# K of group B and q, k of group C made token by token in three products; weights split ahead of the norm's last steps; norm in two steps a tile; PSUM copies moved to ScalarE

## The reference, cut to what matters

```
h = rms_norm(x, norm1)
z = h @ w_in                      # 1024 -> 3072 columns
za, bq, bk, bv, cq, ck, cv, cg = split(z)   # 512, 512, 512, 512, 256, 256, 256, 256
a_out = causal_spatial_gating(gelu(za), ...)      # layer norm of half of za, then a 128x128 mix in time
b_out = dilated_attention(heads(bq), heads(bk), heads(bv))   # 8 heads x 64
c_out = silu(cg) * group_norm(retention(rotary(cq), rotary(ck), cv))   # 4 heads x 64
x = x + concat([a_out, b_out, c_out]) @ w_out
x = x + hier_moe(rms_norm(x, norm2))   # 16 experts, top 2 of one group of 4
```

## Time and profile before

| | us |
|---|---|
| median of 3 runs (lowest, highest) | 730.98 (730.19, 731.46) |
| profiled execution, its own time | 730.64 |
| its span (first to last instruction) | 728.8 |
| PE busy | 684.9 (94%) |
| DVE busy | 285.9 (39%) |
| ACT busy | 178.3 (24%) |
| DMA, mean over the span | 331 GB/s |
| mean granted TensorE clock | 0.988 |

### The profile page before, as it was taken

One profiled execution on the slowest core, in us unless ns is written; L12 is line 12 of the kernel. 1 busy time (PEld: TensorE's weight loads), 2 busy tenths in 40 slices (PEclk: granted clock), 3 DMA queues, 4 the chain that ended last, 5 costly groups with the idle time before them and its releaser, 6 DMA issues.

```text
span 728.8 us, 8951 instructions
## 1 busy us (share of the span) xinstructions
PE 684.9 (94%) x3408; PEld 394.7 (54%) x3408; DVE 285.9 (39%) x583; ACT 178.3 (24%) x332; POOL 16.0 (2%) x29
## 2 busy tenths in 40 slices
PE   6999999899999999997999999989999999998884
PEld 5888778733543543432488878776353453442331
DVE  2439986711231121221453698874121320221224
ACT  3216434211301311101140535442121122101102
POOL 3000000200000000000020000000000000000000
PEclk9999999999999999999999999998999999999998
DMA  9964129999999999999985330897999998999991
GB/s 338 337 237 146 39 99 386 378 387 411 410 418 409 381 420 421 420 420 423 401 277 190 136 116 30 327 389 279 424 402 422 411 424 355 423 421 421 420 411 64
DMA packets 46025, 240.95 MB, mean 331 GB/s; under 512 B 3456, under 2 KB 3648, under 8 KB 21280
## 3 DMA queue, kind: packets, MB, share of 16 engines
q1 hardware_dynamic: 44800, 238.21, 81.3%
q0 software_dynamic: 1040, 2.04, 1.2%
q10 hardware_dynamic: 144, 0.13, 0.1%
HBM read 239.32 MB, written 1.05 MB: 330 GB/s over the span
## 4 chain that ended last, share of the span: by engine, by line
PE 73%; DMA 14%; DVE 9%; ACT 2%; issue 1%; DVEq 0%; SPq 0%; ACTq 0%
PE psum L1012 25%; DMA up_w<-in_w_up 13%; PE psum L715 13%; PE psum L1043 12%; PE psum L735 4%; PE psum L742 4%; PE psum L995 3%; PE psum L956 3%; DVE piece_lo L1111 2%; PE psum L941 1%; PE psum L883 1%; PE psum L700 1%; DVE scores L1148 1%; PE psum L1024 1%; DMA x<-in_x 1%
## 5 line engine op out<-in xcount | busy, mean ns | idle before, releaser
L1012 PE MATMUL psum<-up_w,xT 128*64 128x512 f32 x512 | 113.8, 594 | 8.9 <-DMA up_w<-in_w_up 8.9
L1043 PE MATMUL psum<-down_w,scores 128*64 128x512 f32 x512 | 113.4, 595 | 0.6 <-ACT scores L649 0.6
L715 PE MATMUL psum<-piece_hi,hT_part 128*128 128x512 f32 x288 | 90.6, 396 | 0.6 <-DVE piece_lo L1111 0.6
L1012 PEld LDWEIGHTS psum<-up_w,xT 128*64 128x64 f32 x512 | 37.1, 137 | 82.2 <-issue 66.2
L1443 DVE TENSOR_TENSOR y_lo<-psum,y_hi 128x512 fp32r<-128x512 f32 x32 | 22.1, 692 | 134.1 <-ACT y_hi L656 134.1
L1043 PEld LDWEIGHTS psum<-down_w,scores 128*64 128x64 f32 x512 | 36.6, 137 | 64.6 <-issue 62.4
L1012 PE MATMUL psum<-gate_a,xT 128*64 128x512 f32 x256 | 56.9, 594 | 4.6 <-DMA gate_a<-in_w_gate 4.6
L715 PEld LDWEIGHTS psum<-piece_hi,hT_part 128*128 128x128 f32 x288 | 53.0, 188 | 12.3 <-DVE piece_lo L1111 1.5
L1012 PE MATMUL psum<-gate_b,xT 128*64 128x512 f32 x256 | 56.4, 593 | 0.0
L715 PE MATMUL psum<-piece_lo,hT_part 128*128 128x512 f32 x144 | 56.3, 391 | 0.0
L1428 DVE SCALAR_TENSOR_TENSOR work<-work,psum 128x512 f32<-128x512 f32 x16 | 11.0, 688 | 108.1 <-ACT work L647 108.1
(11 more groups left out here) (240 smaller groups left out, 841.8 us busy)
## 6 DMA issues: line engine op xcount, KB each, us to landing
up_w<-in_w_up SPq DMA_DIRECT2D x32, 2048.0 KB, 13.9
down_w<-in_w_down SPq DMA_DIRECT2D x64, 1024.0 KB, 11.8
gate_b<-in_w_gate SPq DMA_DIRECT2D x32, 1024.0 KB, 13.1
gate_a<-in_w_gate SPq DMA_DIRECT2D x32, 1024.0 KB, 15.4
up_w<-in_w_in SPq DMA_DIRECT2D x6, 2048.0 KB, 11.1
down_w<-in_w_in SPq DMA_DIRECT2D x4, 2048.0 KB, 20.7
down_w<-in_w_out SPq DMA_DIRECT2D x4, 2048.0 KB, 7.8
up_w<-in_w_in SPq DMA_DIRECT2D x4, 1024.0 KB, 8.4
```

Source lines behind the costliest of these rows:

```text
L715: ins = pe.matmul(o, src[a][:, c, t * P:(t + 1) * P], w[b][:, c, :], start=(c == 0 and n == 0), stop=(c == DC - 1 and n == len(parts) - 1))
L1012: ins = pe.matmul(psum[e * SLOTS:(e + 1) * SLOTS, bank, :], xT[:, c, k:k + SLOTS], w[:, e, c, :], start=(c == 0), stop=(c == DC - 1))
L1043: ins = pe.matmul(psum[e * SLOTS:(e + 1) * SLOTS, 2 + n, :], heT[:, c, e * SLOTS:(e + 1) * SLOTS], down_w[:, e, c, n * COLS:(n + 1) * COLS ...
```

## The change

1. BK and CQK go through `three_products` too, tokens on partitions. ACT and DVE split both pieces (4 more halves each; `piece_hi1` is now used by BK, CQK, BV and 7). ACT copies the two token tiles out of PSUM into `vb` with the factor `rstd_in` (`copy_tokens_of`), and PE turns them into features on partitions, 8 transposes each (`turn_tokens`): those of BK between ZA's two token tiles, those of CQK after `turn_probs(0)`. One copy of 1024 columns then takes each result out of PSUM, DVE for K of B, ACT for q and k of C. PE's wait for the masked mixing weights moves ahead of ZA, since the transposes reuse PSUM bank 7.
2. The row of factors is gone with all that made it: `spread`, the product with ones, three DVE products and a copy; the rotary products read the tables themselves.
3. On DVE `norm_probs(0)` stands ahead of the layer norm's last steps, and these are two chained steps on each token tile (four of 128x256) where there were two of 128x256 and two of 128x512. Both low halves of CVG follow each other.
4. The copy of k of C and the middle third of the probabilities' copy go from DVE to ACT.
5. The first `hT` lies in the room of `probsT` (`hT_first`), since the second high buffer covers `hT`.

```diff
-        SPLIT = {ZA: 0, CVG: 1, BV: 2, 6: 3, 7: 4}
-        HI_BUFFER = {ZA: 0, CVG: 0, BV: 1, 6: 0, 7: 1}
-
-        HI_AFTER = {CVG: ZA + 1, BV: CQK + 1, 6: CVG + 1, 7: BV + 1}
+        SPLIT = {BK: 0, ZA: 1, CQK: 2, CVG: 3, BV: 4, 6: 5, 7: 6}
+        HI_BUFFER = {BK: 1, ZA: 0, CQK: 1, CVG: 0, BV: 1, 6: 0, 7: 1}
+
...
+                def copy_tokens_of(j, k):
+
+                    act.wait_ge(projected.sem, projected.at(l, j + 1))
+                    for t in range(T):
+                        ins = act.activation(vb[:, t, :], psum[:, PIECE_BANK[j] + t, :], ACT.Copy, scale=rstd_in[:, t:t + 1])
+                    ins.then_inc(tokens_copied.sem, 1)
+
...
-                    for b in (0, 2):
+                    for b in (range(3) if k == 0 else (0, 2)):
...
-                act.activation(hT_parts[0][:], hT[:], ACT.Copy).then_inc(hT_hi_ready.sem, 1)
+                act.activation(hT_parts[0][:], hT_first, ACT.Copy).then_inc(hT_hi_ready.sem, 1)
+                split_hi(BK)
                 act.wait_ge(projected.sem, projected.at(l, BQ + 1))
                 act.activation(qkb[:, 0:2, :], psum[:, 0:2, 0:SEQ], ACT.Copy).then_inc(proj_copied_a.sem, 1)
                 split_hi(ZA)
+                act.wait_ge(rstd_in_ready.sem, rstd_in_ready.at(l, 1))
+                copy_tokens_of(BK, 0)
+                split_hi(CQK)
                 copy_piece(ZA, za[:, 0, :], rstd_in[:, 0:1])
...
-                copy_piece(CQK, qkc[:, 0:2, :].rearrange("p c t -> p (c t)"))
+                copy_tokens_of(CQK, 1)
                 copy_probs(0)
+                act.wait_ge(tokens_turned.sem, tokens_turned.at(l, 2))
+                act.activation(qkc.rearrange("p c t -> p (c t)"), psum[:, PIECE_BANK[CQK]:PIECE_BANK[CQK] + 2, :].rearrange("p b n -> p (b n)"),
+                               ACT.Copy).then_inc(proj_copied_a.sem, 1)
...
-                    elif j in (BK, CQK):
-
-                        for m in range(4):
-                            o = psum[:, bank + m // 2, (m % 2) * SEQ:(m % 2 + 1) * SEQ]
-                            for c in range(DC):
-                                ins = pe.matmul(o, w[:, c, m * P:(m + 1) * P], hT[:, c, :], start=(c == 0), stop=(c == DC - 1))
-                            if m == 3:
-                                ins.then_inc(projected.sem, 1)
...
+                def turn_tokens(k, bank):
+
+                    pe.wait_ge(tokens_copied.sem, tokens_copied.at(l, k + 1))
+                    for m in range(4):
+                        for t in range(T):
+                            ins = pe.transpose(psum[:, bank + m // 2, (2 * (m % 2) + t) * P:(2 * (m % 2) + t + 1) * P],
+                                               vb[:, t, m * P:(m + 1) * P], ident)
+                    ins.then_inc(tokens_turned.sem, 1)
...
-                pe.wait_ge(spread_ready.sem, spread_ready.at(l, 1))
-                pe.matmul(psum[:, 6, 0:SEQ], C("ones"), spread, start=True, stop=True).then_inc(rstd_spread.sem, 1)
...
-                project(ZA)
+                pe.wait_ge(ws_masked.sem, ws_masked.at(l, 1))
+                project(ZA, lambda: turn_tokens(0, 6))
                 score(0)
                 project(CQK)
                 turn_probs(0)
-
-                pe.wait_ge(ws_masked.sem, ws_masked.at(l, 1))
+                turn_tokens(1, PIECE_BANK[CQK])
+
...
-                link(V.tensor_scalar(q_scale[:], rstd[:, 0:T], HD ** -0.5, None, ALU.mult))
-                V.tensor_tensor(spread.rearrange("p (t q) -> p t q", t=T), C("ident").unsqueeze(1).to_broadcast([P, T, P]),
-                                rstd_in[:].unsqueeze(2).to_broadcast([P, T, P]), ALU.mult).then_inc(spread_ready.sem, 1)
-
-                dve.wait_ge(const_loaded.sem, 16)
+                V.tensor_scalar(q_scale[:], rstd[:, 0:T], HD ** -0.5, None, ALU.mult).then_inc(rstd_in_ready.sem, 1)
 
                 dve.wait_ge(hT_hi_ready.sem, hT_hi_ready.at(l, 1))
-                V.tensor_tensor(hT_parts[1][:], hT[:], hT_parts[0][:].bitcast(F32), ALU.subtract).then_inc(hT_split.sem, 1)
+                V.tensor_tensor(hT_parts[1][:], hT_first, hT_parts[0][:].bitcast(F32), ALU.subtract).then_inc(hT_split.sem, 1)
+                split_lo(BK, 0)
+                split_lo(BK, 1)
                 dve.wait_ge(projected.sem, projected.at(l, BQ + 1))
                 V.tensor_copy(qkb[:, 2:4, :], psum[:, 2:4, 0:SEQ]).then_inc(proj_copied_d.sem, 1)
 
-                dve.wait_ge(rstd_spread.sem, rstd_spread.at(l, 1))
-                link(V.tensor_copy(rstd_row, psum[:, 6, 0:SEQ]))
-                link(V.tensor_tensor(sin_rows, C("sin"), rstd_row, ALU.mult))
+                dve.wait_ge(const_loaded.sem, 16)
                 dve.wait_ge(ws_turned.sem, ws_turned.at(l, 1))
                 V.tensor_tensor(wsT[:], psum[:, 7, :].rearrange("p (g t) -> p g t", g=4),
                                 C("causal").unsqueeze(1).to_broadcast([P, 4, P]), ALU.mult).then_inc(ws_masked.sem, 1)
                 split_lo(ZA, 0)
                 split_lo(ZA, 1)
-                dve.wait_ge(projected.sem, projected.at(l, BK + 1))
-                for n in range(2):
-                    ins = V.tensor_tensor(qkb[:, 4 + 2 * n:6 + 2 * n, :], psum[:, PIECE_BANK[BK] + n, :].rearrange("p (c t) -> p c t", c=2),
-                                          rstd_row.unsqueeze(1).to_broadcast([P, 2, SEQ]), ALU.mult)
-                    if n == 0:
-                        link(ins)
-                ins.then_inc(proj_copied_d.sem, 1)
-                dve.wait_ge(proj_copied_d.sem, proj_copied_d.at(l, BK + 1))
-                V.tensor_tensor(cos_rows, C("cos"), rstd_row, ALU.mult).then_inc(rows_ready.sem, 1)
+                split_lo(CQK, 0)
+                dve.wait_ge(tokens_turned.sem, tokens_turned.at(l, 1))
+                V.tensor_copy(qkb[:, 4:8, :].rearrange("p c t -> p (c t)"), psum[:, 6:8, :].rearrange("p b n -> p (b n)")).then_inc(proj_copied_d.sem, 1)
+                split_lo(CQK, 1)
                 copy_piece(ZA, za[:, 1, :], rstd_in[:, 1:2])
 
                 zf = za.rearrange("p t n -> p (t n)")
@@ -1237,18 +1239,16 @@
                     link(V.bn_aggr(moments[:, t, :], stats[:, t, :]))
                 link(V.tensor_scalar(meansq[:, 0:T], moments[:, :, 1], 4 * EPS, None, ALU.add))
                 link(inverse_roots(T, link))
...
+                norm_probs(0)
+                dve.wait_ge(mix_params_loaded.sem, mix_params_loaded.at(l, mix_params_loaded.turn))
                 for t in range(T):
                     v = za[:, t, A_W:2 * A_W]
-                    ins = V.tensor_scalar(v, v, moments[:, t, 0:1], rstd[:, t:t + 1], ALU.subtract, ALU.mult)
-                    link(ins)
-                v = za[:, :, A_W:2 * A_W]
-                dve.wait_ge(mix_params_loaded.sem, mix_params_loaded.at(l, mix_params_loaded.turn))
-                link(V.tensor_tensor(v, v, ln_g[:].unsqueeze(1).to_broadcast([P, T, A_W]), ALU.mult))
-                V.tensor_tensor(v, v, ln_b[:].unsqueeze(1).to_broadcast([P, T, A_W]), ALU.add).then_inc(vn_ready.sem, 1)
-                norm_probs(0)
+                    link(V.scalar_tensor_tensor(v, v, moments[:, t, 0:1], ln_g[:], ALU.subtract, ALU.mult))
+                for t in range(T):
+                    v = za[:, t, A_W:2 * A_W]
+                    ins = V.scalar_tensor_tensor(v, v, rstd[:, t:t + 1], ln_b[:], ALU.mult, ALU.add)
+                ins.then_inc(vn_ready.sem, 1)
                 split_lo(CVG, 0)
-                copy_piece(CQK, qkc[:, 2:4, :].rearrange("p c t -> p (c t)"))
```

40 lines of the change are left out of this document (18 added, 22 removed).

## The result

The changed kernel takes **723.48 us** (median of 6 runs, 721.76 to 725.34) against 730.08 (six runs, 728.24 to 731.46) for the kernel before: ratio 0.9911, 95% interval 0.9891 to 0.9932. That is 6.5 us less, 5.0 to 8.0. The profiled execution of the changed kernel took 721.76, its span is 720.0.

A forecast was written before the change was run, and what follows sets the result against it. The front was taken as bound by PE to ZA's end, then DVE to CVG's second half. Per layer -0.44 - 2.76 + 0.88 - 1.77 + 0.6 = -3.5; 730.64 - 7.0 = 723.6, plus 0.34: 724.0 us, 8-in-10 range 720.8 to 727.8.

The forecast's parts named there:

- Ones product and BK: PE ahead of ZA: dropping the ones product saves 0.44, BK in three products 2.76; together 3.2 us a layer.
- K's transposes: Eight PE transposes in the middle of ZA cost 0.88 us a layer, at a pitch of 0.11 each.
- The norm's last steps: DVE ahead of CVG: four steps of 256 columns take 1.75 us in place of 2.32, 0.57 less.
- 24 products in a row: CVG's first tile on PE: 5.8 us without a pause, ending at 72.4, takes 0.6 off DVE's gain.
- Behind the swap product: From the swap product on, the order stays the same and everything stands 3.5 us earlier, SP's issue at 100.1 too.
- CQK costs PE 2.9 less, which isn't on the path: PE ahead of CVG: CQK ends at about 62.2 while DVE is busy until 62.6, so its gain becomes waiting.
- The stream ... is started by the front: Experts' weights, 100 MB: an earlier front moves stream and multiplications together, so its gain reaches the layer's end in full.
- The third rival: Experts' stream: it ends when it did, something other than BV's end starting or pacing it; 731, no change; 6 in 100.
- Hidden, by 1.8: Layer 0: ZA's split is done at 37.4; PE wants it from 36.5, the second half 2.7 later, so no wait.
- rival 1: PE's thin stretch ahead of CVG: clock falls to 1.2 GHz for 3.5 us, losing 1.7 a layer; 727.4; 12 in 100.
- The slow side: Low clock holds through CVG's first tile and beyond: 7.0 us per layer takes back all 3.5, 12 gives 736; 4 in 100.
- Rival 4: Routing's lower clock shifts in layer 0, front unchanged: +1.7 (725.7) or -1.7 (722.3); 9 and 9 in 100.

The follow-up runs named there:

- e6: The changed kernel with BK in two products, high by low left out (3.64 us less of PE's time): 720.8 us, ratio 0.9882 to the kernel before.
- e7: The changed kernel with the layer norm's last steps in their old form, two of 128x256 and two of 128x512: 725.7 us, ratio 0.9932 to the kernel before.
- e3: The changed kernel with the copies of C's k and the probabilities' middle third back on DVE, between CVG's two low halves: 725.77 us, ratio 0.9946.
- e4: The changed kernel with a fourth product set in CQK, high by low a second time (3.64 us more of PE's time): 729.64 us, ratio 0.9998.
- e1: The kernel before with only the DVE and ACT edits from ZA's copy on, BK and CQK still in plain float32: 728.70 us against 730.40, ratio 0.9987.
- e10: The changed kernel with SP's issue of the experts' first transfer held until the first half of the attention is done: 723.89 us, ratio 0.9917.
- after_again: The changed kernel run once more, unchanged: 724.53 us, ratio 0.9916 to the kernel before.
- e9: The changed kernel with CVG's first low half split ahead of the norm's last steps and the time mix inside CVG's first tile: 722.51 us, ratio 0.9904.
- e2: The changed kernel with the probabilities' norm behind the layer norm's last steps again: 726.7 us, ratio 0.9965 to the kernel before.
- e5: The changed kernel with CQK in two products, high by low left out (3.64 us less of PE's time): 725.65 us, ratio 0.9939.

## Why the prediction was right, and where it wasn't

**The sum.** 724.0 was forecast and 723.5 measured, -3.5 a layer against -3.25 and -3.45 in the fronts.

- *Ones product and BK.* BK was forecast to take 11.2 from its first product to ZA's and took 11.19 (24.39 to 35.58), with no wait at its own first product, so the bound of 0.8 for its landing is nothing here. e6 shows that such time counts in full where the weights are at hand.
- *K's transposes.* 0.88 forecast, 0.87 measured for eight. The 275 ns that the Trainium skill ("TensorE: Matmul & The Clock Gate", Part 4: PE-mode transpose) gives for a transpose in a kernel is what one takes from start to end, as in the earlier trace rows; eight in a row cost a pitch of 0.11 each.
- *ZA's copy* 2.3 earlier: 2.44 in layer 1, 2.20 in layer 0 from the end of BQ on (25.81 became 23.61).
- *The norm's last steps.* This term was mis-sized. The four steps last from 61.84 to 63.76, 1.92 where 1.75 was forecast, so they save 0.40 of the 2.32 and not 0.57; e7 puts their worth on the path at 0.40 to 0.43 too. The pair with two tensor inputs takes 1.00 and 0.88 (the rows above), not the 0.86 that was taken for it.
- *24 products in a row.* The step that took 0.6 off DVE's gain is right: the first tile runs 5.69 without a pause, and e3 shows that of 1.2 of copies PE sees 0.59. ZA's copy to the swap product was forecast at 24.0 (72.4 - 48.4), counted as in the earlier trace rows, and is 24.16 so counted (71.80 - 47.64; the table's 24.00 goes by the start of the product).
- *Behind the swap product* nothing was to move: 27.80 for 27.83 and 27.88 for 27.88 from there to SP's issue. SP's issue in layer 1 was forecast at 451.2 and stands at 451.25; this one figure is luck in part, since 0.9 of a quicker start (0.8 of it the clock at BQ) and 0.65 lost between the layers lie in it and nearly cancel. In layer 0 it was 99.44 for 100.1.

**Three steps failed, none of which changed the number.**

1. *"CQK costs PE 2.9 less, which isn't on the path ... The gain there goes into waiting."* It is off the path by 1.5 us only (e4). Without the short CQK, DVE's edits bring 0.72 a layer where both together bring 1.0 (e1): the sum was right because it was made for both together. The prediction looked at DVE's chain as it stood before and didn't ask how near PE was: it had one wait of 0.34 there.
2. *"The stream ... is started by the front ... A front that ends earlier moves stream and multiplications together."* The hole from 99 to 102 is there, but it starts nothing that counts: e10 leaves it open and loses nothing. What arrives comes over the chain of work on the engines, and not quite in full: 0.4 to 0.7 of it is lost between the two fronts. The third rival, that the stream would keep its own time, falls with the same run.
3. *"Hidden, by 1.8"*, of ZA's split in layer 0. The prediction set the end of the whole split, 37.4, against the need for the second half; but the first half binds earlier. It comes 4.4 behind the landing (1.93 + 2.31 + 0.14 in after_again's chain). In the profiled executions ZA landed between 30.8 and 32.7, so the first half is ready from 35.2 to 37.1, where PE wants it at 35.2 to 36.2 (earlier where the clock rose sooner in BQ). The cover is 0 to 0.4 in five executions, and in six others with the whole BK PE waits: 0.25 in e9, 0.28 in e2, 0.48 in e4, 0.51 in e3, 1.29 in e5, 1.36 in after_again. The mis-sized thing is both the need (36.5 was taken from an execution with a slow start) and the landing, taken as one number.

**The rivals.** The clock stayed at 1.00 from 61 to 66 in the changed kernel, with PE busy 3.97 of 5: rival 1 didn't come, with pauses of 0.42 and 0.71. e2 and e5 show it with pauses of 2.3 (in one layer of two) and 4.05 (in layer 0; the clock fell in both layers), for 0.6 to 1.7. The slow side, 7 us or more a layer, was seen nowhere in this stretch. The same page of the Trainium skill ("TensorE: Matmul & The Clock Gate", Part 1) tells its source as idle time that brings the clock back to half. That agrees with e5 and e6, and with e2 in one layer and not in the other. Rival 4 came, in one execution: layer 1's routing had 3.4 us at the lower clock, not 7. It makes 1.9 of the profile's 8.8. It is no part of the change, since after_again has 7 us in both layers at the same front of layer 1; how much of it is in the difference of the medians can't be said exactly, and executions with the same mean clock leave 6.0 of the 6.5.

## What to carry to other kernels

Make the sum for the stretch that an edit touches, between two events that both kernels have, and not for spans: here one execution's span was 8.8 shorter, of which the fronts have 6.7 and the change 6.1 at the end. Whether a gain that appears early in a stage reaches its end is a question for one run that delays the thing believed to carry it, here the stream's start; an empty stretch in the DMA row is no evidence that the stream is short. And when several edits shorten one engine's chain, ask after each which engine is next and by how little: e4 and e5 show that 3.64 us more of CQK costs 2.16 of path, and that 3.64 us less gains nothing and leaves PE idle for long enough that the clock falls.
